# Layer 0 of a two-layer decoder trunk: attention batches placed between projections, top-key rounds of both query tiles in turn, and the block compression in fewer, wider matmuls

## What is computed

```python
h = rmsnorm(x)                      # 256 x 1024
a_q, a_lat, i_q, i_k, i_w, b_q, b_kv, b_g = split(h @ w_in)     # 512, 256, 256, 64, 4, 512, 768, 12 columns
# DSA heads (4): one shared key and value from a low-rank latent, keys picked by an indexer
c = rmsnorm(a_lat) * kv_norm;  a_k = c @ w_uk;  a_v = c @ w_uv
isc = sum_h relu(i_q[h] @ i_k.T / 8) * i_w[h];  causal;  keep the 64 largest of every row
oa  = softmax(a_q @ a_k.T * scale + bias, kept keys) @ a_v
# NSA heads (4): three branches, mixed by sigmoid gates
blk  = kv[window of 32 tokens, stride 16] + pos                 # 15 windows, for keys (j=0) and values (j=1)
ck, cv = gelu(blk.reshape(15, 32 * 128) @ w1[j]) @ w2[j]
oc   = softmax(b_q @ ck.T * scale + bias) @ cv                  # "cmp"
osel = softmax(b_q @ sk.T * scale + bias, causal) @ sv          # "sel" (all 4 blocks are selected at 256 tokens)
ow   = softmax(b_q @ wk.T * scale + bias, causal) @ wv          # "win"
x = x + concat(oa, g0 * oc + g1 * osel + g2 * ow) @ w_out
# then: layer 0 dense SwiGLU; layer 1 stick-breaking attention and top-2-of-8 expert SwiGLU; final norm
```

## Time and profile before

| | us |
|---|---|
| median of 3 runs (1498.66 to 1498.9) | 1498.9 |
| the profiled execution | 1502.05 |
| its span, first to last instruction | 1499.9 |
| PE busy, whole span | 1460.3 (97%) |
| DVE busy | 1136.9 (76%) |
| ACT busy | 937.7 (63%) |
| mean granted TensorE clock | 0.99 of full |

### The profile page before, as it was taken

One profiled execution on the slowest core, in us unless ns is written; L12 is line 12 of the kernel. 1 busy time (PEld: TensorE's weight loads), 2 busy tenths in 40 slices (PEclk: granted clock), 3 DMA queues, 4 the chain that ended last, 5 costly groups with the idle time before them and its releaser, 6 DMA issues.

```text
span 1499.9 us, 17248 instructions
## 1 busy us (share of the span) xinstructions
PE 1460.3 (97%) x7186; PEld 1227.4 (82%) x7186; DVE 1136.9 (76%) x848; ACT 937.7 (63%) x731; POOL 33.5 (2%) x37
## 2 busy tenths in 40 slices
PE   8998999999999999999999999999999999999996
PEld 7896678888987888888888888888888888888885
DVE  4486455444645788898898898898899889889885
ACT  3444443443444677777777777777777777777773
POOL 0000000000001000000000000000000000000000
PEclk8999999999999999999999999999999999999998
DMA  9643155554542499999999999999999999999991
GB/s 317 179 142 112 57 196 183 191 174 169 183 161 92 149 383 383 352 363 380 365 360 369 377 368 353 387 356 371 382 354 363 379 361 359 376 374 361 352 381 70
DMA packets 128898, 434.44 MB, mean 290 GB/s; under 512 B 11208, under 2 KB 20400, under 8 KB 113072
## 3 DMA queue, kind: packets, MB, share of 16 engines
q1 hardware_dynamic: 124336, 424.24, 77.6%
q0 software_dynamic: 2016, 7.35, 1.3%
q10 hardware_dynamic: 2464, 1.69, 0.4%
HBM read 431.15 MB, written 2.11 MB: 289 GB/s over the span
## 4 chain that ended last, share of the span: by engine, by line
PE 91%; DVE 5%; ACT 2%; issue 1%; DMA 0%; SPq 0%; POOL 0%; DVEq 0%; ACTq 0%; POOLq 0%
PE ps L1554 28%; PE ps L1556 28%; PE ps L1555 28%; PE ps L2059 2%; DVE lo L1024 1%; PE ps L1616 1%; ACT hi L669 1%; PE ps L1773 1%; PE ps L2004 0%; DVE kv L1136 0%; PE ps L2005 0%; DVE work L1067 0%; DMA raw<-in_ev_w_in_dram 0%; PE ps L1978 0%; DVE top L1135 0%
## 5 line engine op out<-in xcount | busy, mean ns | idle before, releaser
L1024 DVE TENSOR_TENSOR lo<-raw,hi 128x2048 fp32r<-128x2048 f32 (+1 forms) x403 | 903.1, 2283 | 118.3 <-ACT hi L669 117.0
L669 ACT ACTIVATE hi<-raw 128x2048 fp32r<-128x2048 f32 (+1 forms) x403 | 770.7, 1916 | 279.4 <-PE ps L1556 273.2
L1554 PE MATMUL ps<-hi,xT_hi 128*128 128x512 f32 (+2 forms) x1216 | 473.7, 390 | 2.9 <-DVE xT_lo L1210 1.9
L1556 PE MATMUL ps<-hi,xT_lo 128*128 128x512 f32 (+2 forms) x1216 | 468.7, 385 | 0.0
L1555 PE MATMUL ps<-lo,xT_hi 128*128 128x512 f32 (+2 forms) x1216 | 468.1, 385 | 0.0
L1554 PEld LDWEIGHTS ps<-hi,xT_hi 128*128 128x128 f32 x1216 | 229.1, 188 | 49.4 <-DVE xT_lo L1210 2.4
L1556 PEld LDWEIGHTS ps<-hi,xT_lo 128*128 128x128 f32 x1216 | 228.6, 188 | 46.7
L1555 PEld LDWEIGHTS ps<-lo,xT_hi 128*128 128x128 f32 x1216 | 228.9, 188 | 44.2
L1554 PE MATMUL ps<-hi,hT_hi 128*128 128x512 f32 x536 | 210.2, 392 | 0.9 <-DVE hT_lo L1268 0.9
L1556 PE MATMUL ps<-hi,hT_lo 128*128 128x512 f32 x536 | 208.8, 390 | 0.0
L1555 PE MATMUL ps<-lo,hT_hi 128*128 128x512 f32 x536 | 208.6, 389 | 0.0
(11 more groups left out here) (253 smaller groups left out, 850.9 us busy)
## 6 DMA issues: line engine op xcount, KB each, us to landing
raw<-in_od_w_gate_dram SPq DMA_DIRECT2D x112, 1024.0 KB, 7.9
raw<-in_od_w_up_dram SPq DMA_DIRECT2D x112, 1024.0 KB, 7.7
raw<-in_od_w_down_dram SPq DMA_DIRECT2D x112, 1024.0 KB, 7.4
raw<-in_od_w_qkv_dram SPq DMA_DIRECT2D x12, 1024.0 KB, 5.4
raw<-in_ev_w_gate_dram SPq DMA_DIRECT2D x11, 1024.0 KB, 5.6
raw<-in_ev_w_up_dram SPq DMA_DIRECT2D x11, 1024.0 KB, 5.1
raw<-in_ev_w_down_dram SPq DMA_DIRECT2D x11, 1024.0 KB, 5.1
raw<-in_ev_w_in_dram SPq DMA_DIRECT2D x4, 1024.0 KB, 11.0
```

Source lines behind the costliest of these rows:

```text
L669: act.activation(unit(hi, n), unit(raw, n), ACT.Copy).then_inc(hi_ready, 1)
L1024: dve.tensor_tensor(unit(lo, n), unit(raw, n), unit(hi, n).bitcast(F32), ALU.subtract)\
L1554: pe.matmul(out, s_hi, m_hi, start=start, stop=False, skip_group_check=True)
L1556: return pe.matmul(out, s_lo, m_hi, start=False, stop=stop, skip_group_check=True)
```

## The change

It reorders the stage by hand and rewrites the compression.

- Weight units 2 to 9 come in another order: key/value columns (2, 3), NSA queries (4, 5), latent and values (6, 7), DSA queries (8, 9). Each compression unit now holds both `w1` matrices, 8 places each (256 columns instead of 128). The output weights come row half by row half.
- `compress`: the windows lie as four groups of 16 (high and low part, j = 0 and 1) per place, so one stationary window of 64 used rows is multiplied by the 256 columns of `hi` and of `lo`: two matmuls a place, 32 places. DVE copies the 64 x 256 result, and two small matmuls with `fold` sum the four groups and leave it transposed, 128 x 32. There is no transpose of the hidden activations any more, and `gelu` works on 128 x 32.
- `top_rounds(first, last)` runs a round for both tiles in turn and is called in pieces (2, 1, 2, 2, 1 rounds) between the splits.
- Batches are reordered (`sel 0`, `win 0`, `sel 1`, `win 1`, `dsa 0`, `dsa 1`, `cmp 0`, `cmp 1`). The first two run between the projections of units 6 to 9; four more between the compression pieces. A batch is transposed into the PSUM bank of its own scores, tables give the banks.
- `project_out` of the DSA rows (q = 0) for tile 0 stands ahead of the two `cmp` batches' scores, for tile 1 behind them; the NSA rows come last.
- Of the 47 dummy matmuls after 12 us, 13 stay (9 + 4); 11 new ones stand between the diagonal's matmul and the first projection.
- ACT's order follows. One Sqrt now stands between two groups of Exp, so Exp's table is loaded twice.

The diff, cut to its core:

```diff
+    units += k_units(win, [(O_KV, 0, 3 * HD), (O_KV + 4 * HD, 3 * HD, HD)], W)
+    units += k_units(win, [(O_BQ, 0, W)], W)
+    units += k_units(win, [(O_LAT, 0, RANK), (O_KV + 3 * HD, 256, HD), (O_KV + 5 * HD, 384, HD)], W)
     units += k_units(win, [(O_AQ, 0, W)], W)
...
+    for i in range(4):
+        units.append(([(w1[j][:, 8 * i:8 * i + 8], HD * j, HD) for j in range(2)], 8, 2 * HD))
...
+            def top_rounds(first, last):
+                for r in range(first, last):
+                    found = []
+                    for i, t in enumerate((1, 0)):
+                        n = P * (t + 1)
+                        if r == 0:
+                            dve.wait_ge(idx_masked, i + 1)
+                        found.append(mark(dve.max(top8[:, t], (topw if r else iscore)[:, t, 0:n])))
+                    for (t, n), at_count in zip(((1, SEQ), (0, P)), found):
+                        dve.wait_ge(dve_chain, at_count)
+                        taken = mark(dve.match_replace(topw[:, t, 0:n], top8[:, t], (topw if r else iscore)[:, t, 0:n],
+                                                       TAKEN))
+                    dve.wait_ge(dve_chain, taken)
...
             pe.matmul(ps[0:CH, 7, 0:SEQ + P], rel_sb[:], bucket_sb[:], start=True, stop=True).then_inc(diag_done, 1)
+            keep_busy(11, 6)
             project_T(0, 3, 0, (384, 16), norm=0)
...
-                for l in range(16):
-                    place = 16 * q + l
-                    ins = three(ps[:, 7, HD * j:HD * j + HD], blk_window(0, j, place), blk_window(1, j, place),
-                                wh[:, l, :], wl[:, l, :], i == 0 and l == 0, q == 1 and l == 15)
+                for l in range(8):
+                    window = blk_window(8 * i + l)
+                    pe.matmul(ps[:, CMP_BANK, 0:2 * HD], window, wh[:, l, :], start=(i == 0 and l == 0), stop=False)
+                    ins = pe.matmul(ps[:, CMP_BANK, 0:2 * HD], window, wl[:, l, :], start=False, stop=(i == 3 and l == 7))
...
+            project(6, (2, 3), parts=(0,))
+            scores(0)
+            scores(1)
+            project(6, (2, 3), parts=(1,))
+            project_T(8, 4, 0, parts=(0,))
+            batch_probs(0)
+            batch_probs(1)
...
+            project_T(8, 4, 0, parts=(1,))
+            batch_values(0)
+            batch_values(1)
...
+            scores(2)
+            compress(0)
+            scores(3)
+            scores(4)
+            compress(1)
+            batch_probs(2)
+            compress(2)
+            batch_values(2)
+            batch_probs(3)
+            compress(3)
+            batch_values(3)
+            scores(5)
+            batch_probs(4)
+            batch_values(4)
+            fold_hidden()
+            batch_probs(5)
+            batch_values(5)
+            compressed()
+            project_out(0, 0, 0)
+            project_out(0, 1, 0)
```

More of the change, by code:

```diff
@@ L1165, in _ @@
-            for j in range(2):
-                dve.wait_ge(blk_hi_ready, j + 1)
-                dve.tensor_tensor(blk_part(1, j), work[:, 1, W * j:W * j + W], blk_part(0, j).bitcast(F32),
-                                  ALU.subtract).then_inc(blk_ready, 1)
-            splits_to(U_CMP + 3)
-            def gelu():
+            dve.wait_ge(idx_done, 2)
+            splits_to(6)
+            top_rounds(0, 2)
+            splits_to(7)
+            make_windows()
+            top_rounds(2, 3)
@@ new lines, in _ @@
+            dve.wait_ge(small_loaded, 16 * 6)
+            for t in range(T):
+                dve.scalar_tensor_tensor(out=tok[:, t, 0:RANK], in0=tok[:, t, 0:RANK], scalar=stat[:, 6 + t:7 + t],
+                                         in1=kv_gain[:], op0=ALU.mult, op1=ALU.mult).then_inc(lat_ready, 1)
+            splits_to(U_CMP + 1)
+            top_masks()
+            splits_to(U_CMP + 3)
+            logits(2)
+            logits(3)
+            normalise(2)
+            logits(4)
+            splits_to(U_CMP + 4)
@@ L1232, in add_out @@
+            normalise(3)
+            logits(5)
+            normalise(4)
+            copy_parts()
+            normalise(5)
+            gelu_argument()
+            batch_heads(4)
+            gelu_rest()
+            splits_to(U_WO[0] + 1)
+            batch_heads(5)
+            splits_to(U_WO[0] + 2)
+            logits(6)
+            logits(7)
+            normalise(6)
+            normalise(7)
+            splits_to(U_WO[0] + 3)
+            batch_heads(6)
+            batch_heads(7)
             def add_out(layer, i):
@@ L1556, in three, with project_T @@
                 return pe.matmul(out, s_lo, m_hi, start=False, stop=stop, skip_group_check=True)
-            def project_T(first, blocks, bank, extra=None, norm=None):
-                for q in range(2):
+            def project_T(first, blocks, bank, extra=None, norm=None, parts=(0, 1)):
+                for q in parts:
                     n = first + q
@@ L1581, in project_T, with project @@
                     ins.then_inc(units_used, 1)
-            def project(first, banks):
-                for q in range(2):
+            def project(first, banks, parts=(0, 1)):
+                for q in parts:
                     n = first + q
@@ new lines, in _ @@
+            batch_values(0)
+            batch_values(1)
+            pe.wait_ge(latT_copied, 1)
+            for k in range(2):
+                pe.matmul(ps[:, 3, 0:SEQ], wuk[:, k, :], latT[:, k, :], start=(k == 0), stop=(k == 1))
+            for t in range(T):
+                for k in range(2):
+                    ins = pe.matmul(ps[:, 3, SEQ + HD * t:SEQ + HD * t + HD], latT[:, k, P * t:P * t + P], wuv[:, k, :],
+                                    start=(k == 0), stop=(k == 1))
+            ins.then_inc(akv_done, 1)
@@ L1788, in _ @@
+            project_out(0, 0, 0)
+            project_out(0, 1, 0)
+            pe.wait_ge(ckv_copied, 2)
+            scores(6)
+            scores(7)
+            project_out(0, 0, 1)
+            project_out(0, 1, 1)
+            batch_probs(6)
+            batch_probs(7)
+            batch_values(6)
+            batch_values(7)
+            for u in (2, 3):
+                for t in range(T):
+                    project_out(0, u, t)
+            keep_busy(9, 3)
             transpose_tile(1, 0)
-            keep_busy(4, 5)
+            keep_busy(4, 3)
```

372 lines of the change are left out of this document (178 added, 194 removed).

## The result

| | before | changed |
|---|---|---|
| median, us (lowest to highest) | 1498.9 (1498.66 to 1500.41; four executions) | 1488.48 (1486.6 to 1491.28; four) |
| ratio of the times | | 0.9925 [0.9914, 0.9937] |
| profiled execution, us | 1502.05 | 1491.28 |
| its span, us | 1499.9 | 1488.8 |
| its mean granted clock | 0.990 | 0.985 |

The change is faster by 10.4 us (by the interval 9 to 13), beyond the 0.2% that can be told from nothing, and the time lies within the range of 1478 to 1490.5, though outside the band that the forecast itself had (gains of 13.5 to 18.5 us). It is 5.5 us slower than the 1483 forecast. The profiled executions give the same: 10.8 us, where 16 were forecast. All of it is gained in the stage that was changed: from the transposes for the SwiGLU to the end it is 1314.9 us before and 1314.6 now.

What follows compares the result with a forecast made beforehand. PE's work bounds the stage up to 131.5 us, then a PE, DVE, ACT, PE chain. Work -21.7, waits +7.5, clock -1.6: -15.8, with `fold` and tails -16 us; 1486 profiled, 1483 us median, range 1478 to 1490.5.

Steps and rivals of the forecast that it cites:

- the stage moves as a block: Everything behind 185 us keeps its instructions, so what the changed stage saves, the whole kernel saves.
- Compression: Compression matmuls on PE: 192 at 0.112 us become 64 of 256 columns at 0.119, gain 13.9 us (bounds 14.3 to 6.9).
- the dear compression: Rival: each of the 64 compression matmuls takes 0.228 us, 7 us more work; gain 11 us, 1488 us, chance 0.06.
- The new waits: PE's waits in the new order, laid out by hand: 20.8 us against 13.3 before, +7.5 us.
- Rounds: DVE's top-key rounds for both tiles in turn: 1.36 us a pair instead of 1.70, bounds 1.3 and 1.70.
- First dummies: Eleven new dummy matmuls before the first projection: 2.5 us hidden in its wait, full clock from 16.35 to 22.1, worth 2.5.
- The rival of full clock: No half clock behind the long waits or the 16-column matmuls: -20 us, 1479 us, chance 0.10.
- the held half clock: Rival: PE at half clock from the wait at 104 us to near 140 us: gain 9 us, 1490 us, chance 0.13.
- the term of the clock: Half clock on PE costs 6.4 us (two early stretches 2.9, three late 3.5) instead of 8.0: 1.6 us less.
- the dummies: 34 of 47 dummy matmuls removed from PE, 0.228 us each: 7.8 us of work gained.

Runs made afterwards that it cites:

- the second profile: Profile of the changed kernel run again unedited: profiled execution 1489.32 us, with 27.3 us of half-clock time; median 1488.88 us, ratio 0.9929 to the kernel before.
- the reordered kernel: Changed kernel with dsa 1's scores, DVE's normalising of dsa 0, ACT's copy of its probabilities and ACT's unit 12 split moved earlier: 1477.34 us; again 1479.1 us.
- the filled one: Changed kernel with scores, normalising, copy and split moved earlier, plus dummy matmuls in TensorE's remaining waits: 1477.95 us, ratio 0.9835 to the kernel before.

## Why the prediction was right or wrong

**Right:**
- The direction, the range, and that the stage moves as a block (1314.9 and 1314.6 us behind it).
- *Compression.* Steps of 0.12 at full clock, four pieces of 16. Taking 0.119 from the row of the same width was right; 0.228 was not it. The rival of the dear compression falls.
- *The new waits*, each laid out from rows of the old trace: 3.02 us for 3.1, 4.64 for 4.7, 2.46 for 2.8, 1.11 for 1.3, 1.39 for 1.9 (it was 1.14 in the second profile), and around the latent's transposes 0.36, 0.35 and 2.64, together 3.4, for 4.2. In all +7.5 us.
- *Rounds*: 1.29 us, forecast 1.36, bounds 1.3 to 1.70. DVE without idle time from 54.8 to 89 us.
- *First dummies*: hidden in their wait (0.39 us left), full clock behind them.
- *The rival of full clock* (-20 us) was laid out rightly: with the waits filled and one early stretch left, the profiled execution takes 1482.15 us, 19.9 less than before.

The time lies in the range because the range was stretched down to the rival of the held half clock. A small misreading: the earlier trace rows is from a view with 13 waits behind the first, not twelve; their sum of 10.9 us is right.

**Wrong, the term of the clock.** "*one behind each of the long waits, three in all, 3.5: together 6.4, that is 1.6 less*". The two early stretches are there, and so are three late ones, each beginning in a long wait, but they last 6.75, 6.75 and 17.25 us and cost 2.3, 0.85 and 4.3 us, 7.5 instead of 3.5. The waits (+7.5) came as laid out. With the work as booked the sum is then -21.7 + 7.5 + 2.4 = -11.8 us, where 2.4 is the clock (2.9 + 7.5 against 8.0 before), and -10.8 was measured: 4 of the 5 us that are missing are the clock's, about 1 us stays unexplained. Filling the five waits took 7 us away, which shows it on the chip.

Where did the step go wrong? I had taken the length of a stretch from the old trace, 3.3 us (once 6.8), and there nearly every stretch was followed by a busy PE. The 17 us stretch lies across three waits with little between them: PE is busy 11.3 of 17.25 us. I had listed just that as what would make me wrong: half clock for over a third of 104 to 140 us. It is 60% (48% in the second profile):

```profile
104.00:140.00 36.00, 24.76 (x108) 18.20 (x107) 21.57 (x31) 15.63 (x40) 0.00 (x0) 0.70 0.19 59
```

So the rival *half clock held through the gaps* (-9 us, 1490, chance 0.13) came out in the main: between 108.5 and 140 us the clock was at full only from 115.25 to 125.5 us. The measured -10.8 is nearer to it than to the -16 of the forecast, whose own range ended at -13.5. The 0.13 was too low, and the argument against it was one window at 138 us where the clock rose in a part with gaps. The same trace falls back to half at 141.5 us: of 134.5 to 145.5 us, with PE busy 8.71 of 11, nearly two thirds are at half clock. I had its cost in the sum and left it out of the argument.

```profile
134.50:145.50 11.00, 8.71 (x27) 5.41 (x26) 6.96 (x7) 5.19 (x14) 0.00 (x0) 0.69 0.38 125
```

The Trainium skill, page TensorE: Matmul & The Clock Gate, section Part 1: The HAM clock gate, says that the throttled state is the default and activity releases it. The 17 us stretch agrees with that; the second profile's 104 to 122 us, at full clock with PE busy 11.63 of 18 us, shows that gaps alone did not always bring the half clock.

**Wrong in its parts, right in the sum: the dummies.** "*34 go: 34 x 0.228 = 7.8 us*" counts them as work on the path. The old order without them is 10 us slower. They lay there mostly in would-be waits, and held the clock. The sum survived since the layout of the new order counted every wait afresh (a dummy that is gone shows up there as a wait); as an account of what each edit brings it was wrong.

**Wrong: what the first dummies are worth** (2.5 us; measured 0, give or take some 2), and **what the rounds are worth** (1.1 us reaching the end; about 3 us of waits, since the wait before `sel 1` does not absorb DVE's delay).

**The compression's gain** of 13.9 us is right as work of PE, but not as time: with 6.4 us of it put back, the time does not change by more than the intervals tell. Between 95 and 140 us PE is not the bound throughout, so a good part of that gain was bought back as waits, 3 to 4 us of them seen. Those waits were in the layout; what was missing against the forecast is the clock.

Left open: why in some executions half clock appears at 22 to 40 us, with PE busy 98% of the time, and in others not at all.

## What to carry to other kernels

Removing TensorE work behind which VectorE and ScalarE set the pace turns into gaps, and a gap can be paid twice: once as a wait, once as matmuls at half clock behind it. Lay out the new waits from the old rows (that worked to a few tenths here), then treat gaps that follow each other closely as one stretch of half clock from the first wait to the end of the last, not as one short stretch each. And before counting dummy matmuls as work to be saved, ask what would stand in their place; the better cure for a gap is an order that has no gap: moving one batch's scores, one normalising, one copy and one split here gave 11.5 us more, and dummies added to that at most 3.

## What the runs showed of the hardware

- The same program at different granted clocks. Ten executions of the reordered kernel run from 1476.25 us (mean clock 0.994) to 1483.73 (0.988); five of the filled one from 1473.79 (0.996) to 1479.82 (0.991). The long waits in the two profiles of the first are the same. What differs is where half clock falls, also in a part where PE has no wait. It goes with 6 to 7.5 us of 1478 here, more than half of what the studied change brings. An effect of a few us asks for the mean clock of each run beside its time. The Trainium skill, page TensorE: Matmul & The Clock Gate, section Part 1: The HAM clock gate, says of the slow matmuls at a kernel's start that their number varies from run to run; in these runs it is stretches in the middle that vary.
- A stretch of half clock prevented at one place is not yet time gained: without the first dummies it fell at 16.8 to 20.2 us, with them at 23.25 to 26.5 us, and the time was the same.
- Half clock costs 0.43 us per us where PE is the bound (13.7 us, 5.9 us), and less where it waits: from the latent's transposes to the second output piece the changed kernel's first profile (86.27 to 146.66 us, PEclk 0.76) has about 9 us more of it than its second (84.66 to 143.37, 0.83) and takes 1.7 us longer.
- At full clock, each with a load of weights, matmuls start 0.11 us apart with 16 columns (29.12 and 29.23 us in the changed kernel), 0.112 with 128, 0.119 with 256 and 0.228 with 512. Up to 256 columns the count of matmuls is what is paid here.
